# A fused transformer kernel on one core: where the first expert's weights are loaded

## The chip, the core and the metric

The kernel runs on one core of a Trainium2 chip. The metric is device time in microseconds (us). One execution was also recorded by the hardware profiler; every single event below comes from that execution. The engines are TensorE (PE: matmuls, PEld: its weight loads), VectorE (DVE), ScalarE (ACT), GpSimd (POOL) and SyncE (SP). SP here only issues weight loads; 16 DMA engines carry them out.

## What is computed

One hybrid layer on 256 tokens of width 1024, followed by a second block. In outline:

```python
proj = rmsnorm(x, g_mix) @ w_in
y_a = moba_attention(...)        # 8 heads
y_b = causal_attention(...)      # 8 heads, the "mla" branch
merged = sigmoid(gate_a) * (y_a @ w_branch_a) + sigmoid(gate_b) * (y_b @ w_branch_b)
x = x + merged @ w_out
x = x + routed_experts(rmsnorm(x, g_ffn), ...)   # 32 experts, top 4
x = x + sigmoid(rmsnorm(x, g_ple) @ w_ple_gate) * (p @ w_ple_proj)
# then a second block: swiglu, a mixer, memory attention, swiglu, rmsnorm
```

All weights are float32 in HBM. Each expert has 8 MB of gate-and-up weights and 4 MB of down weights, and all 32 experts are loaded, about 384 MB of the 544 MB that the kernel reads.

## The kernel before

The engines' programs are written out by hand, one function each (`tensor`, `scalar`, `vector`, `gpsimd`, `sync`), and run in the written order; semaphores tie them together. Weights are cut into **parts**: 1 MB each for the attention's matrices (`w_branch_a` and `w_branch_b` have two each, `w_out` four), 2 MB each for the experts (`gate_up` four parts, `down` two per expert).

`Plan.place` gives each part a place and makes the list of loads. There are five ring places of 2 MB, a place X behind them, a place Y in the work memory (both for experts only), and two odd ones: APART holds expert 0's fourth gate_up part in two pieces of 1 MB, ASIDE its first down part in pieces of 0.5 and 0.25 MB. A part goes to the place whose holder is the oldest. SP walks through the list in `load_before`: it waits until PE has used up the place's last holder (`pe["w", k]`), then issues the load. It is in order: a wait holds up every load behind it.

An attention part is not used as it lands. ACT first casts it to fp32r into the place's other half (`hi`, L1424), then DVE makes the rest (`lo`, L2012); PE needs both. ACT does this where its program says `hi_to(n)`, DVE at `lo_to(n)`. Parts 19, 20 and 21 are the second half of `w_branch_a` and the two of `w_branch_b`; parts 22 to 25 are `w_out`. Expert parts are used as they land.

The end of the attention goes, on PE: gate 3, branch_a 0, the transposes of the mla probabilities, branch_a 1 (L592 to L594), the mla values (L753, L754), branch_b 0, branch_b 1 with the transposes of the merged rows 0 and 1 (`merged_t`), out 0 (L611 to L613), out 1, the router. On ACT: `values` evacuates the mla values (L1466), `hi_to(24)` follows, then `merged_T(0)`, `merged_T(1)` (L1583). On DVE: `branch_b(0, h)`, `lo_to(22)`, `branch_b(1, 0)` (L2246, L2248), the rests of merged rows 0 and 1 (L2026). POOL waits for the mla values and then loads the experts' biases and the router (five transfers, 1 MB in all).

In the experts PE computes gate_up of expert n, then down of expert n-1. The load of an expert's part waits for a place that a part about 1.5 experts earlier gives up: the second gate_up part of expert 3 for the first of expert 2, for example.

Of the kernel before, what the change touches and what calls it, by code (L numbers as in the profile page):

```python
# [19 lines left out]
C_ID, C_CM, C_LT, C_NGE, C_ONE, C_IOTA, C_RC, C_RS, C_MC, C_MS, C_SEL, C_HM = (  # L20
    0, 128, 256, 384, 512, 640, 704, 768, 832, 864, 896, 928)
# [75 lines left out]
class Plan:  # L97
# [67 lines left out]
    def place(self):  # L165


        first, crowded, behind = (self.of[k][0] for k in (("gate_up", 0), ("gate_up", CHECK), ("ple_gate", 0)))
        self.apart, self.aside = self.of["gate_up", 0][3], self.of["down", 0][0]
        self.slot, self.at, self.loads = {}, {}, []  # L170
        count = dict.fromkeys(range(ASIDE + 1), 0)
        held = {s: s - NS for s in range(NS)}
        i = 0
        while i < len(self.parts):
            if i == first:
                held[X], held[Y] = self.of["out", 1][1] - 0.5, self.of["out", 1][1] + 0.5
            if i == crowded:
                del held[Y]
            if i == behind:
                del held[X]  # L180
            oldest = sorted(held, key=held.get)
            slots = oldest[:1]
            if i in (self.apart, self.aside):
                slots = [APART if i == self.apart else ASIDE]
            elif self.joined(i) and max(oldest[:2]) <= X and abs(oldest[0] - oldest[1]) == 1:
                slots = sorted(oldest[:2])
            after = [held[s] for s in slots if held.get(s, -1) >= 0]
            count[slots[0]] += {APART: 2, ASIDE: 5}.get(slots[0], 1) * 16
            for k, s in enumerate(slots):
                self.slot[i + k], self.at[i + k] = s, (slots[0], count[slots[0]])  # L190
                if s in held:
                    held[s] = i + k
            self.loads.append((i, len(slots), after))
            i += len(slots)
        early = next(n for n in self.loads if n[0] == self.apart)
        self.loads.remove(early)
        self.loads.insert(1 + [n[0] for n in self.loads].index(first), early)

    def on_vector(self, i):

# [47 lines left out]
def build(nc, d, out, known):  # L248
# [3 lines left out]
    with ExitStack() as ctx:  # L252
# [42 lines left out]
        def W(o, *shape):  # L295
            return view(Wt, o, shape)
# [47 lines left out]
        def raw_chunk(i, kk):  # L344

            if i == plan.apart:
                return (W(6144, 2048), W(10240, 2048))[kk]
            return chunks(raw(i), i)[:, kk, :]

        def down_half(i, kk, dh):  # L350
# [1063 lines left out]
        def scalar(e):  # L1414
            made = [0]

            def hi_to(i):

                while made[0] <= i:
                    j = made[0]  # L1420
                    made[0] += 1
                    if parts[j].split:
                        e.wait_ge(*in_memory(j))
                        e.copy(hi(j), raw(j)).then_inc(*act.now(("hi", j)))  # L1424
# [151 lines left out]
                probs_T("mla", g)  # L1576
            hi_to(21)
            values("mla", yT[1])
            hi_to(24)

            def merged_T(i):
                e.wait_ge(*pe["merged_t", i])
# [2 lines left out]

            for i in range(2):
                merged_T(i)
            hi_to(25)
            for i in (2, 3):
                merged_T(i)  # L1590
            e.wait_ge(bgu_in, 48)
            e.copy(bgub[0:96, :], bgu[0:96, :]).then_inc(*act.now("bias_hi"))
            e.activation(table_out, ident[:, 0:1], ACT.Sqrt).then_inc(*act.now("table0"))
            for q0 in (32, 64):
                e.wait_ge(*dve["bias_1", "rest"])
                e.copy(bgub[q0:q0 + 32, :], bgu[q0:q0 + 32, :]).then_inc(*act.now(("bias_1", q0)))
# [1265 lines left out]
        def sync(e):  # L2862
            e.dma_start(x[:, 0, :], d["x"][0:128, :]).then_inc(x_in0, 16)
            e.dma_start(x[:, 1, :], d["x"][128:256, :]).then_inc(x_in1, 16)
            made = [0]

            def load_before(i):

                while made[0] < len(plan.loads) and plan.loads[made[0]][0] < i:
                    j, n, after = plan.loads[made[0]]  # L2870
                    made[0] += 1
                    p, w = parts[j], d[parts[j].name]
                    for k in after:
                        e.wait_ge(*pe["w", k if k in plan.slot else of["out", 1][1]])
                    if p.name in PACKED:
                        src = w[p.c0 // p.n].rearrange("p (k n) -> p k n", k=p.k)
                    elif p.expert < 0:
                        src = rows(w, p.k0, p.k, p.c0, p.n)
                    elif p.name == "w_gate_up":
                        src = w[p.expert][p.k0 * 128:(p.k0 + p.k) * 128, :].rearrange("(p k) n -> p k n", p=128)  # L2880
                    else:
                        src = w[p.expert][p.k0 * 128:(p.k0 + p.k) * 128, :].rearrange("(p k) n -> p k n", p=128)
                    if j == 0:
                        e.dma_start(chunks(raw(0), 0)[:, 0:2, :], src[:, 0:2, :]).then_inc(first_in, 16)
                        e.dma_start(chunks(raw(0), 0)[:, 2:4, :], src[:, 2:4, :]).then_inc(loaded[0], 16)
                    elif j == plan.apart:
                        e.wait_ge(*pe["merged_t", 3])
                        for kk in range(2):
                            e.dma_start(raw_chunk(j, kk), src[:, kk, :]).then_inc(loaded[APART], 16)
                    elif j == plan.aside:  # L2890
                        e.wait_ge(*pe["logits"])
                        e.wait_ge(*act["bias_2", 64])
                        for k, v in enumerate((cst[:, C_HM:C_HM + 1024], W(12288, 1024), W(14336, 1024))):
                            e.dma_start(v, src[:, k, :]).then_inc(loaded[ASIDE], 16)
                        for c in range(2):
                            e.dma_start(aside[3][c], src[:, 3, c * 512:(c + 1) * 512]).then_inc(loaded[ASIDE], 16)
                    elif j == tail:
                        for k in range(3):
                            e.dma_start(chunks(raw(j), j)[:, k, :], src[:, k, :]).then_inc(tail_in[k], 16)
                        e.dma_start(chunks(raw(j), j)[:, 3, :], src[:, 3, :]).then_inc(in_memory(j)[0], 16)  # L2900
                    elif n == 2:
                        s = plan.slot[j]
                        e.dma_start(ring_t[:, s * SLOT:(s + 2) * SLOT].rearrange("p (k n) -> p k n", n=p.n),
                                    src).then_inc(in_memory(j)[0], 16)
                    else:
                        if plan.slot[j] == Y:
                            e.wait_ge(*pe["logits"])
                            e.wait_ge(*act["bias_2", 64])
                        e.dma_start(chunks(raw(j), j), src).then_inc(in_memory(j)[0], 16)
# [76 lines left out]
```

## Time and profile before

| | |
|---|---|
| median of 3 runs | 1754.18 us (1752.94 to 1755.97) |
| span of the profiled execution | 1754.0 us |
| PE busy | 1650.0 us (94%) |
| DMA moved | 546.39 MB, mean 312 GB/s |
| DMA rate in the 21 slices from 175 to 1096 us | 423 to 429 GB/s |
| chain that ended last | PE 48%, DMA 30% |

How to read the rows further down. A row of the stretches gives start:end and length, then busy us and instruction count of PE, PEld, DVE, ACT and POOL, the clock granted to PE (1.00 is 2.4 GHz, 0.50 is 1.2 GHz), the busy share of the DMA engines and their GB/s. A row of the timeline gives start, length, engine (SPq is SP's queue), line, operation, output<-input, shapes and count; idle time before it and what ended it stand in brackets. A row of the DMA issues gives output<-input, issuer, count, KB each and median us from issue to landing. A row of the waits gives who waited for whom, us in total, times, and the longest.

### The profile page before, as it was taken

To read this page: it belongs to the slowest core of one execution; us is meant where nothing else is said; L and a number is where in the kernel's file an instruction comes from. 1 tells how busy PE (TensorE), PEld (TensorE's weight loads), DVE (VectorE), ACT (ScalarE), POOL (GpSimd) and SP (SyncE) were. 2 spreads that over 40 slices of the span, in tenths; PEclk is the share of its full clock that TensorE was granted. 3 is DMA by queue.
4 is the path that set the end of the run, shared out by engine and by line. 5 is a ranking of instruction groups with operands and counts; after the bars stand their busy time and mean duration, and the time that the engine had idled before them with its cause. 6 is when DMAs were issued, how large, how long until landed. Compare 5 with 4: busy or idle time off the path is not lost.

```text
span 1754.0 us, 20351 instructions
## 1 busy us (share of the span) xinstructions
PE 1650.0 (94%) x8885; PEld 1037.7 (59%) x8886; DVE 705.4 (40%) x879; ACT 572.4 (33%) x790; POOL 24.5 (1%) x37
## 2 busy tenths in 40 slices
PE   9999999798889999988888888999999999999998
PEld 7788533342344544533232333388888998988886
DVE  5897411121212112111020111177664865567653
ACT  7576200111111111100000001175554765455552
POOL 1000000000000000000000000000000000000000
PEclk9999999999999999999999999999999999999999
DMA  7537999999999999999999999945555424445552
GB/s 250 171 120 294 424 423 429 426 427 428 428 426 427 428 426 427 426 427 428 429 427 427 429 424 428 400 159 192 192 192 172 164 97 135 164 136 179 191 192 96
DMA packets 119354, 546.39 MB, mean 312 GB/s; under 512 B 5776, under 2 KB 64272, under 8 KB 93696
## 3 DMA queue, kind: packets, MB, share of 16 engines
q1 hardware_dynamic: 117936, 540.96, 77.3%
q0 software_dynamic: 1040, 4.00, 0.7%
q8 instruction: 72, 1.18, 0.3%
q14 instruction: 18, 0.15, 0.0%
q10 hardware_dynamic: 288, 0.11, 0.0%
HBM read 544.00 MB, written 1.05 MB: 311 GB/s over the span
## 4 chain that ended last, share of the span: by engine, by line
PE 48%; DMA 30%; DVE 1%; ACT 1%; issue 1%; DVEq 0%; ACTq 0%
DMA ring<-in_w_down 30%; PE PS L1023 9%; PE PS L640 8%; PE PS L1182 6%; PE PS L647 4%; PE PS L982 2%; PE PS L625 1%; PE PS L626 1%; PE PS L627 1%; PE PS L1197 1%; PE PS L592 1%; PE PS L594 1%; PE PS L593 1%; PE PS L1225 1%; PE PS L664 1%; PE PS L666 1%
## 5 line engine op out<-in xcount | busy, mean ns | idle before, releaser
L982 PE MATMUL PS<-ring,work 128*64 128x512 f32 x1984 | 439.9, 595 | 29.8 <-DMA ring<-in_w_gate_up 29.7
L2012 DVE TENSOR_TENSOR ring<-ring,ring 128x2048 fp32r<-128x2048 f32 (+2 forms) x129 | 286.9, 2233 | 246.6 <-ACT ring L1424 246.5
L982 PEld LDWEIGHTS PS<-ring,work 128*64 128x64 f32 x1984 | 137.6, 137 | 311.9 <-issue 245.8
L1424 ACT CAST ring<-ring 128x2048 fp32r<-128x2048 f32 (+2 forms) x130 | 241.0, 1864 | 199.0 <-DMA ring<-in_mem_w_kv 85.5
L1023 PE MATMUL PS<-ring,work 128*64 128x512 f32 x992 | 235.7, 620 | 50.5 <-DMA ring<-in_w_down 35.8
L1023 PEld LDWEIGHTS PS<-ring,work 128*64 128x64 f32 x992 | 74.4, 141 | 197.0 <-issue 160.6
L2449 DVE TENSOR_SCALAR work<-PS 128x512 f32<-128x512 f32 x32 | 22.1, 690 | 321.0 <-PE PS L982 321.0
L1688 ACT ACTIVATE work<-work 128x512 f32<-128x512 f32 x32 | 20.2, 630 | 360.8 <-DVE work L2449 360.8
L2345 DVE TENSOR_TENSOR work<-PS,work 128x512 fp32r<-128x512 f32 x32 | 22.1, 692 | 253.7 <-ACT work L1631 253.7
L1182 PE MATMUL PS<-ring,work 128*128 128x512 f32 x432 | 98.2, 390 | 0.0
L1182 PEld LDWEIGHTS PS<-ring,work 128*128 128x128 f32 x432 | 81.2, 188 | 16.8
L640 PE MATMUL PS<-ring 128*128 128x512 f32 x320 | 75.2, 391 | 0.5 <-DVE ring L2503 0.5
L640 PE MATMUL PS<-work,ring 128*128 128x512 f32 x320 | 75.2, 391 | 0.5 <-DVE work L2503 0.5
L1631 ACT CAST work<-PS 128x512 fp32r<-128x512 f32 x32 | 18.8, 586 | 159.5 <-PE PS L1023 159.5
L640 PEld LDWEIGHTS PS<-work,ring 128*128 128x128 f32 x320 | 59.3, 188 | 13.0 <-DVE work L2503 1.4
L640 PEld LDWEIGHTS PS<-ring 128*128 128x128 f32 x320 | 59.3, 188 | 13.1 <-DVE ring L2503 1.4
L592 PE MATMUL PS<-ring 128*128 128x512 f32 (+1 forms) x160 | 62.9, 393 | 0.3
L593 PE MATMUL PS<-ring 128*128 128x512 f32 (+1 forms) x160 | 61.8, 386 | 0.0
L594 PE MATMUL PS<-ring 128*128 128x512 f32 (+1 forms) x160 | 61.8, 386 | 0.0
L924 PEld LDWEIGHTS PS<-work 128*128 128x128 f32 x256 | 34.0, 202 | 24.3 <-issue 23.5
L924 PE MATMUL PS<-work 128*128 128x256 f32 x256 | 40.3, 302 | 0.0
L647 PEld LDWEIGHTS PS<-ring 128*128 128x128 f32 x320 | 39.7, 192 | 0.8
(446 smaller groups left out, 2338.6 us busy)
## 6 DMA issues: line engine op xcount, KB each, us to landing
ring<-in_w_gate_up SPq DMA_DIRECT2D x124, 2048.0 KB, 21.6
ring<-in_w_down SPq DMA_DIRECT2D x61, 2048.0 KB, 21.4
ring<-in_ffn_w_gu SPq DMA_DIRECT2D x44, 1024.0 KB, 5.1
ring<-in_w_in SPq DMA_DIRECT2D x27, 1024.0 KB, 5.3
ring<-in_ffn_w_down SPq DMA_DIRECT2D x22, 1024.0 KB, 4.9
ring<-in_w_out SPq DMA_DIRECT2D x8, 1024.0 KB, 5.3
ring<-in_mem_w_kv SPq DMA_DIRECT2D x8, 1024.0 KB, 16.9
work<-in_w_gate_up SPq DMA_DIRECT2D x3, 2048.0 KB, 16.4
```

The costliest lines, as they stand in the source:

```text
L592: e.matmul(o, lT[0][:, k, hs], whi[:, kk, :], start=k == 0, stop=False, skip_group_check=True)
L593: e.matmul(o, lT[0][:, k, hs], wlo[:, kk, :], start=False, stop=False, skip_group_check=True)
L594: t = e.matmul(o, lT[1][:, k, hs], whi[:, kk, :], start=False, stop=k == nk - 1, skip_group_check=True)
L640: t = e.matmul(PS[:, bank + j, :], whi[:, k, j * 128:(j + 1) * 128], rT[2][:, :, k, :], start=first and k == 0, stop=not first and k == 7, ...
L647: t = e.matmul(PS[:, bank + j, 0:256], wlo[:, k, j * 128:(j + 1) * 128], rT[0][:, k, :], start=first and k == 0, stop=not first and k == 7 ...
L924: t = e.matmul(PS[:, bank, c * 256:(c + 1) * 256], half[:, h, 256 * i + c:256 * i + 256:2], PGr[:, h, :], start=h == 0 and z == 0, stop=h ...
L982: t = e.matmul(PS[hf * 64:hf * 64 + 64, bank, :], XG[g % 2][:, 2 * kp + kk, i * 64:(i + 1) * 64], raw_chunk(w, kk)[:, c0 + hf * 512:c0 + h ...
L1023: t = e.matmul(PS[dh * 64:dh * 64 + 64, BDN, :], HT[:, kk, kp * 64:kp * 64 + 64], down_half(w, kk, dh), start=kp == 0 and kk == 0, stop=kp ...
L1182: t = e.matmul(PS[:, 4 + 2 * h + nb, :], hT[z][:, c, hs], chunks(half, w)[:, kk, nb * 512:(nb + 1) * 512], start=c == 0 and q == 0, stop=F ...
L1424: e.copy(hi(j), raw(j)).then_inc(*act.now(("hi", j)))
L2012: e.tensor_tensor(lo(j), raw(j), hi(j).bitcast(F32), ALU.subtract).then_inc(*dve.now(("lo", j)))
L2345: e.tensor_tensor(YRl, PS[:, BDN, :], YRh.bitcast(F32), ALU.subtract).then_inc(*dve.now(("YR", n)))
```

## The change

Two of expert 0's gate_up parts, and pieces of two others, are loaded earlier, among the attention's last parts.

- `place` gives the two ring places that gate 2 leaves to expert 0's first two gate_up parts (4 MB). The attention's last seven parts (branch_a 1, branch_b 0 and 1, the four of w_out) turn over the three places that are left; each is loaded later than before.
- APART's two pieces are issued apart: piece 1 once the mla scores are done, ahead of branch_a 1's load; piece 0 after `merged_t` 3, ahead of the last w_out load. Piece 1 moves from W(10240) to W(10048).
- ASIDE's pieces: 0 and half of 3 without a wait ahead of expert 0's first load; 1 and 2 after the mla values and ahead of out 0's first load; the other half of 3 after the biases.
- ACT's `hi_to(24)` ahead of the merged rows becomes `hi_to(22)`; 23 and 24 come behind the two `merged_T` pairs, 25 behind the bias cast.

```diff
@@ place @@
+        begin, early = self.of["branch_a", 1][0], self.of["gate_up", 0][:2]
         while i < len(self.parts):
+            if i == begin:
+                for j in early:
+                    s = min(held, key=held.get)
+                    count[s] += 16
+                    self.slot[j], self.at[j] = s, (s, count[s])
+                    self.loads.append((j, 1, [held.pop(s)]))
             if i == first:
+                held.update((self.slot[j], j) for j in early)
+                i = early[-1] + 1
...
-        early = next(n for n in self.loads if n[0] == self.apart)
-        self.loads.remove(early)
-        self.loads.insert(1 + [n[0] for n in self.loads].index(first), early)
+        self.loads = [n for n in self.loads if n[0] not in (self.apart, self.aside)]
@@ scalar @@
             values("mla", yT[1])
-            hi_to(24)
+            hi_to(22)
...
             for i in range(2):
                 merged_T(i)
-            hi_to(25)
+            hi_to(23)
             for i in (2, 3):
                 merged_T(i)
+            hi_to(24)
             e.wait_ge(bgu_in, 48)
...
+            hi_to(25)
@@ sync @@
+            def beside_loads(j):
+
+                if j == of["gate_up", 0][0]:
+                    load_aside(0)
+                    load_aside(3, 0)
+                if j == of["branch_a", 1][0]:
+                    e.wait_ge(*pe["mla", "scores"])
+                    load_apart(1)
+                if j == of["out", 0][0]:
+                    e.wait_ge(*pe["mla", "values", 1])
+                    load_aside(1)
+                    load_aside(2)
+                if j == of["out", 1][1]:
+                    e.wait_ge(*pe["merged_t", 3])
+                    load_apart(0)
+                if j == of["down", 0][1]:
+                    e.wait_ge(*act["bias_2", 64])
+                    load_aside(3, 1)
```

SP's queue from the first load of branch_a to the last load of w_out. Before:

```order
L2909 DMA ring_49<-in_w_branch_a 128x4x512 [waits pe_attention_done] x2
L2909 DMA ring_49<-in_w_branch_b 128x4x512 [waits pe_attention_done] x2
L2909 DMA ring_49<-in_w_out 128x4x512 [waits pe_attention_done] x4
L2909 DMA ring_49<-in_w_gate_up 128x4096 [waits pe_attention_done]
L2889 DMA work_51<-in_w_gate_up 128x2048 [waits pe_attention_done]
L2889 DMA work_51<-in_w_gate_up 128x2048
L2909 DMA ring_49<-in_w_gate_up 128x4096 [waits pe_attention_done] x5
```

The same place in SP's queue after the change:

```order
L2942 DMA ring_49<-in_w_branch_a 128x4x512 [waits pe_attention_done]
L2887 DMA cst_55<-in_w_down 128x1024
L2889 DMA more_60<-in_w_down 128x512
L2942 DMA ring_49<-in_w_gate_up 128x4096 [waits pe_attention_done] x2
L2881 DMA work_51<-in_w_gate_up 128x2048 [waits pe_attention_done]
L2942 DMA ring_49<-in_w_branch_a 128x4x512 [waits pe_attention_done]
L2942 DMA ring_49<-in_w_branch_b 128x4x512 [waits pe_attention_done] x2
L2887 DMA work_51<-in_w_down 128x1024 [waits pe_attention_done]
L2887 DMA work_51<-in_w_down 128x1024
L2942 DMA ring_49<-in_w_out 128x4x512 [waits pe_attention_done] x3
L2881 DMA work_51<-in_w_gate_up 128x2048 [waits pe_attention_done]
L2942 DMA ring_49<-in_w_out 128x4x512 [waits pe_attention_done]
```

The expert loads have moved in among those of the attention, and the first three loads of w_out now stand behind a wait for the mla values and two pieces of w_down.

ACT from the evacuation of the mla values (L1466 before, L1473 after) to the bias cast; `ring0` read into `ring1` by a CAST is a `hi`, PS into `ring1` a merged row. Before:

```order
L1466 CAST work1_52<-PS 128x512 [waits pe_attention_done] x2
L1424 CAST ring1_50<-ring0_49 128x2048 [waits ring2_loaded]
L1424 CAST ring1_50<-ring0_49 128x2048 [waits ring3_loaded]
L1424 CAST ring1_50<-ring0_49 128x2048 [waits ring4_loaded]
L1583 CAST ring1_50<-PS 128x512 [waits pe_attention_done] x2
L1424 CAST ring1_50<-ring0_49 128x2048 [waits ring0_loaded]
L1583 CAST ring1_50<-PS 128x512 [waits pe_attention_done] x2
L1592 CAST work2_53<-work0_51 96x2048 [waits b_gu_loaded]
```

The same place on ACT after the change:

```order
L1473 CAST work1_52<-PS 128x512 [waits pe_attention_done] x2
L1431 CAST ring1_50<-ring0_49 128x2048 [waits ring1_loaded]
L1590 CAST ring1_50<-PS 128x512 [waits pe_attention_done] x2
L1431 CAST ring1_50<-ring0_49 128x2048 [waits ring2_loaded]
L1590 CAST ring1_50<-PS 128x512 [waits pe_attention_done] x2
L1431 CAST ring1_50<-ring0_49 128x2048 [waits ring3_loaded]
L1600 CAST work2_53<-work0_51 96x2048 [waits b_gu_loaded]
```

One cast of w_out is left ahead of the first two merged rows, in ring place 1; the others stand behind them. DVE's and PE's order is the same in both kernels.

## Rows read from the trace of the kernel before

**Rows 1.** The page's chain that ended last, share of the span by engine.

```profile
PE 48%; DMA 30%; DVE 1%; ACT 1%; issue 1%; DVEq 0%; ACTq 0%
```

**Rows 2.** The chain in order of time, start, length: one expert's wait.

```profile
392.07 26.92 DMA ring<-in_w_down
```

**Rows 3.** Stretches: PE, PEld, DVE, ACT, POOL busy; PE's clock; DMA share; GB/s.

```profile
120.00:145.00 25.00, 24.81 (x142) 20.72 (x141) 18.24 (x22) 19.73 (x44) 1.20 (x3) 1.00 0.47 166
145.00:150.00 5.00, 5.00 (x24) 4.12 (x23) 3.89 (x4) 4.55 (x3) 1.72 (x3) 1.00 0.90 222
...
160.00:180.00 20.00, 20.00 (x99) 16.70 (x97) 13.14 (x13) 11.78 (x15) 0.00 (x0) 1.00 1.01 429
200.00:240.00 40.00, 40.00 (x202) 15.63 (x200) 9.00 (x18) 4.04 (x8) 1.72 (x3) 1.00 1.01 429
...
241.00:246.00 5.00, 5.00 (x26) 1.64 (x24) 0.00 (x0) 0.00 (x0) 0.00 (x0) 1.00 0.99 374
...
400.00:500.00 100.00, 84.72 (x422) 31.30 (x420) 15.59 (x32) 12.62 (x25) 0.00 (x0) 1.00 1.01 427
```

**Rows 4.** PE's waits, total, times, longest: 100 to 186 us, then 186.7 to 336.

```profile
PE PS L910 <- DVE work L2318: 0.6, 1, 0.6
...
PE PS L1023 <- DMA ring<-in_w_down: 1.4, 2, 1.2
```

**Rows 5.** Timeline of SP's queue: start, length, what it issues.

```profile
127.20 0.37 SPq L2909 DMA_DIRECT2D ring<-in_w_branch_b  x1
...
155.78 0.34 SPq L2909 DMA_DIRECT2D ring<-in_w_gate_up  x1
...
162.15 11.21 SPq L2909 DMA_DIRECT2D ring<-in_w_gate_up  x3
...
241.39 0.33 SPq L2909 DMA_DIRECT2D ring<-in_w_gate_up  x1
```

**Rows 6.** DMA issues at 127.20, 143.80 to 144.80, 155.78 and 241.39: issue to landing.

```profile
ring<-in_w_branch_b SPq DMA_DIRECT2D x1, 1024.0 KB, 5.0
...
work<-in_b_gate_up POOLq DMA_DIRECT2D x3, 256.0 KB, 4.9
...
ring<-in_w_gate_up SPq DMA_DIRECT2D x1, 2048.0 KB, 7.6
...
ring<-in_w_gate_up SPq DMA_DIRECT2D x1, 2048.0 KB, 8.4
```

**Rows 7.** Timeline of ACT: the casts, the mla values, the merged rows.

```profile
128.53 1.98 ACT L1424 CAST ring<-ring 128x2048 fp32r<-128x2048 f32 x1
...
143.54 0.59 ACT L1466 CAST work<-PS 128x512 fp32r<-128x512 f32 x1 [0.72 <-PE PS L754]
144.02 5.53 ACT L1424 CAST ring<-ring 128x2048 fp32r<-128x2048 f32 x3
```

**Rows 8.** Timeline of DVE: rest of a part, branch_a 0, branch_b 1, merged rests.

```profile
130.55 2.29 DVE L2012 TENSOR_TENSOR ring<-ring,ring 128x2048 fp32r<-128x2048 f32 x1 [0.34 <-ACT ring L1424]
132.76 1.28 DVE L2229 TENSOR_TENSOR work<-PS,work 128x512 f32<-128x512 f32 x2
...
152.99 0.68 DVE L2246 TENSOR_TENSOR work<-PS,work 128x512 f32<-128x512 f32 x1
...
154.32 1.28 DVE L2026 TENSOR_TENSOR ring<-PS,ring 128x512 fp32r<-128x512 f32 x2
```

**Rows 9.** Timeline of PE: branch_a 1 begins; out 0 begins.

```profile
134.99 0.48 PE L592 MATMUL PS<-ring,work 128*128 128x512 f32 x1
...
155.59 0.39 PE L611 MATMUL PS<-ring 128*128 128x512 f32 x1
```

**Rows 10.** Timeline of PE, 16 matmuls each: after a short pause, after a long one.

```profile
498.12 3.65 PE L982 MATMUL PS<-ring,work 128*64 128x512 f32 x16 [1.24 <-DMA ring<-in_w_gate_up]
505.59 5.35 PE L1023 MATMUL PS<-ring,work 128*64 128x512 f32 x16 [3.81 <-DMA ring<-in_w_down]
```

**Rows 11.** Stretch right after that long pause, columns as in group 3.

```profile
507.00:510.20 3.20, 3.20 (x10) 1.20 (x8) 0.58 (x1) 0.00 (x0) 0.00 (x0) 0.50 1.02 435
```

More of the change, by code:

```diff
@@ L346, in raw_chunk @@
             if i == plan.apart:
-                return (W(6144, 2048), W(10240, 2048))[kk]
+                return (W(6144, 2048), W(10048, 2048))[kk]
             return chunks(raw(i), i)[:, kk, :]
@@ L2865, in sync, with rows_of, load_apart, load_aside @@
             made = [0]
+            def rows_of(j):
+                p = parts[j]
+                return d[p.name][p.expert][p.k0 * 128:(p.k0 + p.k) * 128, :].rearrange("(p k) n -> p k n", p=128)
+            def load_apart(kk):
+                e.dma_start(raw_chunk(plan.apart, kk), rows_of(plan.apart)[:, kk, :]).then_inc(loaded[APART], 16)
+            def load_aside(k, c=None):
+                src = rows_of(plan.aside)
+                if k < 3:
+                    v = (cst[:, C_HM:C_HM + 1024], W(12288, 1024), W(14336, 1024))[k]
+                    e.dma_start(v, src[:, k, :]).then_inc(loaded[ASIDE], 16)
+                else:
+                    e.dma_start(aside[3][c], src[:, 3, c * 512:(c + 1) * 512]).then_inc(loaded[ASIDE], 16)
+            def beside_loads(j):
[15 more added lines that the diff above has]
+                    load_aside(3, 1)
             def load_before(i):
@@ L2871, in load_before @@
                     made[0] += 1
+                    beside_loads(j)
                     p, w = parts[j], d[parts[j].name]
@@ L2885, in load_before @@
                         e.dma_start(chunks(raw(0), 0)[:, 2:4, :], src[:, 2:4, :]).then_inc(loaded[0], 16)
[L2886 to L2896, printed above, removed]
                     elif j == tail:
```

## The prediction

> **What bounds the kernel now.** I read the chain first, then the stretches, then the waits of PE and of SP's queue. The chain gives DMA 30% of the span [rows 1], in pieces like the 26.92 us of one expert at 392 us [rows 2]. The stretches say why: from 160 us on the 16 DMA engines are full and move 427 to 429 GB/s, while PE is idle for 15 of 100 us at 400 to 500 us [rows 3]. Before that, from 120 to 145 us, they move 166 GB/s [rows 3]. So a reader would start the expert stream earlier, in the attention's idle DMA time. At 427 GB/s 1 MB (1.049 million bytes) takes 2.46 us.
>
> But from when is the stream alone the bound? PE's waits answer: between 100 and 186 us it waits 0.6 us for one thing, and between 186.7 and 336 us only 1.4 us for a weight [rows 4]. Up to about 320 us PE is the one that runs without a pause, and loads go out when PE gives up places. I therefore look for the point where DMA has least queued work. A 2 MB load into a quiet queue takes 7.6 us (issued at 155.78), one that stands behind others takes more; the load issued at 241.39 took 8.4 us [rows 5, 6]. At 241.39 there was at most 0.8 us of queued work left (part of it a load of POOL's), although the stream had run for 85 us. The stretch from 241 to 246 us has 374 GB/s instead of 429 [rows 3]: a small hole is there already.
>
> **Part 1, the earlier stream.** The load at 241.39 goes out when PE has used up expert 2's first part, and this dependence isn't changed. If PE gets there at the same time, every byte that could be queued before is landed, and the stream restarts from that release whatever it had in hand. A lead of any size shrinks to the work that stood queued there: between nothing (the hole) and 0.8 us. I take a gain of 0.8 us. The 18 MB in nine places can be full sooner; nobody asks for them sooner. What the loads cost on SP is small: three more issues below 0.5 us each.
>
> It follows that PE's time of arrival in the experts counts in full. Any delay of PE in the attention moves the release at 241.39, and the DMA stream, then bound to the end of the experts, moves with it. So the rest is about PE in the attention, which had no slack there [rows 4].
>
> **Part 2, branch_a 1.** Its load was made long before; now it waits for gate 3's place, which comes free at 127.20 (where SP issued branch_b 1 before) [rows 5]. It lands 5.0 us later [rows 6], at 132.2. ACT stands at this cast at 128.53 already [rows 7] and holds its queue (the sigmoid of gate 3, the cast of branch_b 0, the probabilities). The cast takes 1.98 us, to 134.2; DVE's rest 2.29, to 136.5; then DVE has the first half of branch_a 0 to evacuate, 0.64 us [rows 8], and PE, which began at 134.99 [rows 9], begins at about 137.2. **+2.2 us.** The values, their evacuation (ACT at 143.54 [rows 7]) and branch_b move along: the values are done at 145.7.
>
> **Part 3, out 0.** SP now issues two 0.5 MB pieces after the mla values and only then out 0's first part; its own place is free earlier. Its landing is not shown by the trace. Lower bound: 2 MB from 145.8 in a quiet queue land in 7.6 us [rows 6], at 153.4. POOL issues its 1 MB at the same moment. In the trace these bytes had the engines to themselves and kept them 90% busy at 222 GB/s for most of 5 us [rows 3], the bias loads landing after 4.9 us [rows 6]. Shared at full rate they add 2.5 us, at their own rate 4.5 us: 155.9 or 157.9. I take 156.5, nearer the first, since mixed traffic at 241 us kept 374 GB/s.
>
> The rule that bears on this is in the Trainium skill, DMA: Bandwidth & Descriptors, Queues, rings and completion order: an engine takes turns between the queues that have work, packet by packet. By that rule POOL's megabyte delays out 0; by plain order of issue it would come behind and the landing would be 153.4.
>
> Now the queues behind it. ACT has this one cast ahead of the merged rows: 1.84 us (three took 5.53 [rows 7]). DVE has the rest of the part, 2.3 us, ahead of branch_b (1, 0), 1.33 us from its start to the merged rests, and the first merged rest is half of 1.28 us [rows 8]. With the hand-overs that is 6.3 us from landing to the start of out 0 on PE: 162.8 instead of 155.59 [rows 9]. **+7.2 us in all**, part 2's 2.2 included; with the bounds +4.1 and +8.6. Moving two casts behind the merged rows saves ACT 3.7 us, but only time that ACT had, since the rows waited for PE.
>
> **Part 4, the rest of out.** Out 0's second part can be loaded when branch_b 0 is done (about 151.7), out 1's first when branch_b 1 is (158): both are landed by 163, before PE wants them at 169 and 175. The last part waits for out 0's first (162.15 before [rows 5], now 170 to 171), so it is ready 5.1 + 1.9 + 2.3 = 9.3 us later, while PE has two parts ahead of it. Places came free every 5.4 us there (three issues from 162.15 within 11.21 us [rows 5]), so that is 10.9 us. It fits by 1.5 us; without this cover each further us of lateness would be one on PE. APART's second piece is issued 3 us ahead and is gone by then. I cost it at nothing. The router, the biases and place Y then come later along with PE.
>
> **Part 5, the clock.** PE stands still from the end of branch_b 1 at 157.7 to 162.8, about 5 us. After a pause of 3.81 us the trace shows the granted clock at 0.50 (1.2 GHz) for the next stretch [rows 10, 11], and 16 matmuls take 5.35 instead of 3.65 us: **+1.7 us**. Bounds: nothing, and 3.4 us if the 2.2 us pause of part 2 costs as much.
>
> **Sum.** 7.2 + 1.7 - 0.8 = +8.1 us on an execution of 1754.0 us, which lies 0.2 us under the median of 1754.18: **1762.3 us**. Since PE and the stream both move by this and nothing is changed after the first experts, it stays to the end.
>
> **Rivals.** (A) The stream is the bound from its start. Then 4 MB, APART's first piece and 0.75 MB of ASIDE leave it, and one w_out part (1 MB) comes in: 4.75 MB, 11.7 us, 1742.5 us. For it: 427 GB/s without a break from 160 us. Against: the latency of 8.4 us at 241.39, and PE without waits up to 320 us. A page backs it, the Trainium skill, Perfetto Trace Analysis, Optimization Strategy: a kernel with several regimes may gain when they are interleaved. By that rule the result is rival A; the trace agrees that there are two regimes, but also shows the places, not the engines, in charge between them. (B) The attention isn't delayed after all, because the late parts find PE still busy: then part 1 alone is left, 1753.4 us. For it speaks only that three places of 5.4 us work each are 16 us, more than the 9.3 us of load and casts; against, the wait for the values that stands ahead of out 0. (C) Out 0 lands at its lower bound and the clock stays up: +4.1 - 0.8, 1757.5 us. (D) POOL's bytes cost 4.5 us, both pauses cost clock and no backlog is won: +8.6 + 3.4 = +12, 1766.2 us. (E) The expected order doesn't bite, as the 4 MB themselves are issued late: they need gate 2's places, free at about 104 us, and land by 117, so this I exclude.
>
> **How the numbers follow.** Forecast 0.50, A 0.06, B 0.10, C 0.19, D 0.15. 0.2% is 3.5 us, about what a measurement of this kernel can tell from no change: within it fall B and about a third of C (its time lies just at the edge); faster is A. That gives faster 0.07, same 0.17, slower 0.76. The range takes in C and D, 1756.5 to 1767, and leaves out A, B and a little at each end, under 0.2.
>
> **What would show it.** (1) PE waits at branch_a 1 for DVE's rest, about 2 us, at 135. (2) PE waits at out 0 (about 5 us, on DVE's merged rest), and DVE and ACT wait there for the landing of w_out, 9 to 11 us after its issue near 146.8. (3) The clock is 0.50 for some us behind it. (4) DMA is idle for several us between 160 and 245, and the load of expert 3's second part goes out near 250 with a latency of about 7.6 us. (5) From there on everything stands 8 us later. I am wrong if out 0 starts before 160, or if a load goes out at 241 without a delay and the end still moves.

## The result, and the profile after

| | before | after |
|---|---|---|
| median, 4 runs each | 1753.76 us (1752.94 to 1755.97) | 1769.01 us (1768.42 to 1769.67) |
| span of the profiled execution | 1754.0 us | 1767.4 us |

The ratio is 1.0084, with a 95% interval of 1.0073 to 1.0096: the change costs 15.25 us, against 8.1 forecast. The direction was right and the size was not; 1769.0 lies above the range of 1756.5 to 1767.

The page's chain looks as it did [rows 1]:

```profile
PE 46%; DMA 31%; DVE 1%; ACT 1%; issue 0%; DVEq 0%; ACTq 0%
```

SP's queue through the attention's end, and the load that answers to the one at 241.39 [rows 5]. Columns as there:

```profile
127.21 0.38 SPq L2942 DMA_DIRECT2D ring<-in_w_branch_a  x1
...
147.33 0.83 SPq L2887 DMA_DIRECT2D work<-in_w_down  x2
148.20 0.43 SPq L2942 DMA_DIRECT2D ring<-in_w_out  x1
...
257.05 0.33 SPq L2942 DMA_DIRECT2D ring<-in_w_gate_up  x1
```

From issue to landing, for the loads at 127.21, 147.72, 148.20 and 257.05:

```profile
ring<-in_w_branch_a SPq DMA_DIRECT2D x1, 1024.0 KB, 5.0
...
work<-in_w_down SPq DMA_DIRECT2D x1, 512.0 KB, 11.0
...
ring<-in_w_out SPq DMA_DIRECT2D x1, 1024.0 KB, 13.9
...
ring<-in_w_gate_up SPq DMA_DIRECT2D x1, 2048.0 KB, 7.7
```

branch_a 1 behaves as a 1 MB load alone. Out 0's first part does not: 13.9 us for the same megabyte, landed at 162.1. The load at 257.05 goes out 15.66 us later than the one at 241.39 did and lands 14.9 us later; 7.7 us is the latency of a quiet queue [rows 6].

ACT stands in front of both late parts (timeline, as in group 7):

```profile
132.26 1.90 ACT L1431 CAST ring<-ring 128x2048 fp32r<-128x2048 f32 x1 [3.51 <-DMA ring<-in_w_branch_a]
...
147.34 0.59 ACT L1473 CAST work<-PS 128x512 fp32r<-128x512 f32 x1 [0.71 <-PE PS L761]
...
162.08 1.90 ACT L1431 CAST ring<-ring 128x2048 fp32r<-128x2048 f32 x1 [14.15 <-DMA ring<-in_w_out]
```

DVE's rest of that part, branch_b (1, 0) and the merged rests follow as in group 8:

```profile
164.01 2.29 DVE L2021 TENSOR_TENSOR ring<-ring,ring 128x2048 fp32r<-128x2048 f32 x1 [9.37 <-ACT ring L1431]
166.22 0.68 DVE L2255 TENSOR_TENSOR work<-PS,work 128x512 f32<-128x512 f32 x1
167.55 1.28 DVE L2035 TENSOR_TENSOR ring<-PS,ring 128x512 fp32r<-128x512 f32 x2
```

and PE starts branch_a 1 at 137.14 and out 0 at 168.38, where it had started at 134.99 and 155.59 [rows 9]:

```profile
137.14 0.50 PE L599 MATMUL PS<-ring,work 128*128 128x512 f32 x1 [1.90 <-DVE work L2238]
...
168.38 0.77 PE L618 MATMUL PS<-ring 128*128 128x512 f32 x1 [8.86 <-DVE ring L2035]
```

The first matmul takes 0.77 us instead of 0.39: the clock. The stretches of the kernel after, columns as in group 3:

```profile
138.00:141.30 3.30, 3.30 (x9) 2.59 (x8) 3.08 (x3) 3.30 (x6) 0.00 (x0) 0.50 0.00 0
...
150.00:158.00 8.00, 8.00 (x42) 6.69 (x40) 3.53 (x5) 0.00 (x0) 0.52 (x1) 1.00 1.01 249
...
168.40:172.00 3.60, 3.60 (x9) 2.83 (x10) 3.56 (x4) 0.00 (x0) 0.00 (x0) 0.50 0.00 0
...
199.40:206.20 6.80, 6.25 (x28) 4.34 (x29) 5.59 (x16) 2.60 (x4) 1.55 (x2) 0.50 1.00 425
...
400.00:500.00 100.00, 86.10 (x438) 33.43 (x436) 21.42 (x45) 15.58 (x32) 1.71 (x3) 1.00 1.01 427
```

Three stretches at half clock (1.2 GHz), one behind each pause and one in the router. Between 120 and 250 us the kernel before had only the last, and half as long:

```profile
186.00:189.30 3.30, 3.30 (x14) 2.57 (x13) 2.52 (x6) 1.39 (x2) 1.54 (x2) 0.50 0.99 420
```

From 150 to 158 us the engines are full (share 1.01) at 249 GB/s; in the same kernel they are as full at 427 GB/s from 400 on. And that last row is the row of before [rows 3]: in the steady part nothing has changed. So the whole loss is made before 206 us. In steps, each the difference of the two traces: branch_a 1 +2.15, the mla values +3.8 (ACT's evacuation at 147.34 instead of 143.54), out 0 +12.8, the release of expert 3's second gate_up part +15.7, its landing +14.9. The spans differ by 13.4, the medians by 15.25. A span is about 1.8 us shorter than the time of its execution (1767.4 for 1769.17 after), so the profiled execution of the kernel before took some 1755.8 us, 2 us above its median. It has a half-clock stretch at the end of the experts (16 matmuls in 5.35 us at 1119.82) where the same 16 took 3.65 us after, which is 1.7 us of this.

### The profile page after: what moved, and what is told of

Same layout as the page of the kernel before. It is cut to its first block, busy times and chain, and to the rows that moved or that the text cites. A ratio compares the mean times of both kernels' runs of the same rounds, so it can differ in the third digit from the quotient of the medians.

```text
span 1767.4 us, 20350 instructions
## 1 busy us (share of the span) xinstructions
PE 1647.5 (93%) x8885; PEld 1037.5 (59%) x8886; DVE 705.7 (40%) x879; ACT 572.7 (32%) x790; POOL 24.6 (1%) x37
## 3 DMA queue, kind: packets, MB, share of 16 engines
HBM read 544.00 MB, written 1.05 MB: 308 GB/s over the span
## 4 chain that ended last, share of the span: by engine, by line
PE 46%; DMA 31%; DVE 1%; ACT 1%; issue 0%; DVEq 0%; ACTq 0%
DMA ring<-in_w_down 31%; PE PS L1030 9%; PE PS L647 8%; PE PS L1189 6%; PE PS L654 4%; PE PS L989 2%; PE PS L632 1%; PE PS L633 1%; PE PS L634 1%; PE PS L1204 1%; PE PS L599 1%; PE PS L601 1%; PE PS L600 1%; PE PS L1232 1%; PE PS L671 1%; PE PS L673 1%
## 5 line engine op out<-in xcount | busy, mean ns | idle before, releaser
L989 PE MATMUL PS<-ring,work 128*64 128x512 f32 x1984 | 441.6, 597 | 34.8 <-DMA ring<-in_w_gate_up 34.8
L2021 DVE TENSOR_TENSOR ring<-ring,ring 128x2048 fp32r<-128x2048 f32 (+2 forms) x129 | 287.0, 2234 | 271.5 <-ACT ring L1431 271.3
L1030 PE MATMUL PS<-ring,work 128*64 128x512 f32 x992 | 226.9, 600 | 51.2 <-DMA ring<-in_w_down 37.8
L647 PE MATMUL PS<-ring 128*128 128x512 f32 x320 | 75.2, 391 | 0.5 <-DVE ring L2512 0.5
L647 PEld LDWEIGHTS PS<-ring 128*128 128x128 f32 x320 | 59.2, 188 | 13.1 <-DVE ring L2512 1.4
L618 PE MATMUL PS<-ring 128*128 128x512 f32 x80 | 32.4, 405 | 10.4 <-DVE ring L2035 8.9
```

The lines of the kernel that those rows point to most:

```text
L618: e.matmul(o, lT[0][:, k, hs], whi[:, kk, :], start=k == 0, stop=False, skip_group_check=True)
L647: t = e.matmul(PS[:, bank + j, :], whi[:, k, j * 128:(j + 1) * 128], rT[2][:, :, k, :], start=first and k == 0, stop=not first and k == 7, ...
L989: t = e.matmul(PS[hf * 64:hf * 64 + 64, bank, :], XG[g % 2][:, 2 * kp + kk, i * 64:(i + 1) * 64], raw_chunk(w, kk)[:, c0 + hf * 512:c0 + h ...
L1030: t = e.matmul(PS[dh * 64:dh * 64 + 64, BDN, :], HT[:, kk, kp * 64:kp * 64 + 64], down_half(w, kk, dh), start=kp == 0 and kk == 0, stop=kp ...
L2021: e.tensor_tensor(lo(j), raw(j), hi(j).bitcast(F32), ALU.subtract).then_inc(*dve.now(("lo", j)))
```

## The experiments

The theory: the loss is PE's delay in the attention, carried over by the release at 241.39, and the lead of the early bytes is worth nothing there. The rivals: the stream itself bounds (a lead counts, a delay of PE is absorbed); or the turning over of three places costs the time, not the wait and the pieces ahead of out 0. Every run is compared with the kernel before on the same chip. "Release" is the issue of expert 3's second gate_up part, 241.39 before and 257.05 after.

**1. Only a delay of PE.** The kernel before, with products of zeros for some 10 us ahead of the experts.

```diff
             tok_part(xT, of["out", 1], 1, 1, PS[:, 3, :], ("out", 1, 1))
+            idle_products(7, 44)
             pe.stage("experts")
```

> The kernel before, with 44 products of zeros (about 0.23 us each, 10.0 us together, bank 7, results unused) on PE between the last w_out matmul and the router. No load, place or order is changed. Theory T (from PE's arrival in the experts on, loads go out as PE gives up places, and the stream has under 1 us of queued work at 241 us): the whole kernel is later by 10.0 less 0 to 0.8 us, +9.2 to +10.0 us; the load of 241.39 goes out near 251 with a latency near 7.6 us. Rival (the stream of weights is the bound from 160 us on): PE's 10 us are hidden, within +-1 us of the kernel before.

1764.0 us, ratio 1.0055 (1.0038 to 1.0071), +9.9 us. SP's queue and the landing of the released load:

```profile
251.97 0.33 SPq L2910 DMA_DIRECT2D ring<-in_w_gate_up  x1
...
ring<-in_w_gate_up SPq DMA_DIRECT2D x1, 2048.0 KB, 8.0
```

The release moved by 10.6 us, the end by 9.9. The full queue of loads absorbed nothing. This is the step that the forecast rested on, and it stands.

**2. The wait and the two pieces away from out 0.** After, with both moved behind `merged_t` 3.

```diff
-                if j == of["out", 0][0]:
-                    e.wait_ge(*pe["mla", "values", 1])
-                    load_aside(1)
-                    load_aside(2)
                 if j == of["out", 1][1]:
                     e.wait_ge(*pe["merged_t", 3])
+                    load_aside(1)
+                    load_aside(2)
                     load_apart(0)
```

> The changed kernel, but the wait for the mla values and the two 0.5 MB pieces of w_down stand behind merged_t 3 (with APART's piece) instead of ahead of out 0's first load. Theory T: out 0's first part goes out at about 145 and lands at 150 to 152, PE doesn't wait at out 0; what is left is the pause at branch_a 1 and its clock loss, 3.6 us, less up to 0.8: +2.8 to +3.6 us against the kernel before. Rival (three places are too few, whatever stands ahead of out 0): still +8 us or more.

1761.2 us, ratio 1.0040 (1.0026 to 1.0054), +7.1 us. Half of the loss is gone, but not as much as expected, a miss. Out 0's first part landed after 5.0 us. PE's waits from 100 to 200 us show why: DVE's rest at L2021 is that of w_out's last part, which was now queued behind 2 MB of pieces. My edit had made a wait of its own.

```profile
PE PS L618 <- DVE ring L2021: 2.6, 1, 2.6
PE PS L599 <- DVE work L2238: 2.3, 1, 2.3
```

**3. The same, with the pieces behind all of w_out.**

```diff
-                if j == of["out", 0][0]:
-                    e.wait_ge(*pe["mla", "values", 1])
+                if j == of["gate_up", 0][2]:
+                    e.wait_ge(*pe["merged_t", 3])
                     load_aside(1)
                     load_aside(2)
-                if j == of["out", 1][1]:
-                    e.wait_ge(*pe["merged_t", 3])
                     load_apart(0)
```

> As out_unblocked (+7.1 us), but the two pieces of w_down and APART's piece 0 stand behind w_out's last load, which had PE waiting 2.97 us there. Theory T (only PE's pauses and the clock after them count): the pause at branch_a 1 is left, 2.2 + 1.4 us, less up to 0.8: +2.8 to +3.6 us. Rival (three places cost more than their pauses): still +7 us.

1757.9 us, ratio 1.0020 (1.0011 to 1.0030), +3.6 us. Only the pause at branch_a 1 is left:

```profile
PE PS L599 <- DVE work L2238: 1.8, 1, 1.8
```

So the part of the loss at out 0 is 15.3 - 3.6 = 11.7 us. What half clock adds is in this difference: the trace of this run has none behind the pause at branch_a 1, after has. The release is at 243.89, 2.5 us late.

**4. Without the early 4 MB.** After, with `early` empty: the seven parts have all five places.

```diff
-        begin, early = self.of["branch_a", 1][0], self.of["gate_up", 0][:2]
+        begin, early = self.of["branch_a", 1][0], []
...
-                i = early[-1] + 1
```

> The changed kernel without its early 4 MB: expert 0's first two parts stand at their old place in the list and attention has five places again; the pieces, SP's waits and ACT's order stay as in the change. Theory T (the wait for the mla values and the 1 MB ahead of out 0 make the delay): out 0's first part is issued at about 144.5 and lands near 158; PE begins out 0 near 164.5, 9 us late, plus 1.9 us of clock, less 0.8: +10 us. Rival (the turning over of three places makes it): PE isn't late, within 1 us of the kernel before.

1765.9 us, ratio 1.0072 (1.0055 to 1.0089), +11.8 us. The pause at branch_a 1 is gone, out 0's first part still took 14.2 us, and PE waited for it:

```profile
PE PS L617 <- DVE ring L2034: 9.2, 1, 9.2
```

The three places don't make the delay of out 0; the wait for the values and the pieces do. 11.8 here and 3.6 in experiment 3 add up to the whole, 15.3.

**5. Each of the two suspects at out 0 apart.** First POOL's megabyte moved out of the way, behind the first merged rows:

```diff
             e.wait_ge(*pe["mla", "values", 1])
+            e.wait_ge(*pe["merged_t", 1])
             for i in range(3):
```

> The changed kernel with POOL's five loads (1 MB) behind merged_t 1 instead of at the mla values. Their sharing of the engines is out of the way of out 0. Theory T: the three loads issued from 147.3 on land as 2 MB in a quiet queue do, after 7.6 to 8.1 us (162.06 in the changed kernel), PE begins out 0 near 162 instead of 168.4: +9 us against the kernel before. Rival (the two pieces of w_down and the w_out part are slow by themselves): still about +15 us.

1762.5 us, ratio 1.0054 (1.0039 to 1.0070), +8.0 us. Out 0's load, issued at 146.83, and PE's wait for it:

```profile
ring<-in_w_out SPq DMA_DIRECT2D x1, 1024.0 KB, 8.2
...
PE PS L618 <- DVE ring L2035: 3.2, 1, 3.2
```

It lands at 155.0 instead of 162.1. From the first of the three issues that is 9.1 us instead of 14.7: POOL's 1 MB alone had cost out 0 5.6 us. The kernel ends 7.3 us earlier. Some 1.4 us of that isn't POOL's: in this execution the stretch behind the pause at branch_a 1 is at full clock, and the mla values are done earlier by as much (first issue at 145.96 instead of 147.33).

Then the wait kept where it is, and only the two pieces moved behind `merged_t` 3:

```diff
                     e.wait_ge(*pe["mla", "values", 1])
-                    load_aside(1)
-                    load_aside(2)
                 if j == of["out", 1][1]:
                     e.wait_ge(*pe["merged_t", 3])
+                    load_aside(1)
+                    load_aside(2)
                     load_apart(0)
```

> The changed kernel with SP's wait for the mla values kept ahead of out 0, but the two 0.5 MB pieces behind merged_t 3. Theory T: out 0's part is issued at 147.3, with POOL's 1 MB beside it; at the 0.25 MB/us seen when both ran together it lands near 158, 4 us sooner than in the changed kernel: +11 us. Rival (the wait alone is the cost, the 1 MB ahead costs nothing): +15 us.

1769.5 us, ratio 1.0085 (1.0070 to 1.0101), +15.0 us, a miss. Out 0's part landed 9.6 us after its issue, and the pause ahead of it did shrink: PE began out 0 at 162.2, 6 us earlier than after. But the pieces stood ahead of w_out's last part again, as in experiment 2, and PE paused there:

```profile
PE PS L618 <- DVE ring L2035: 3.7, 1, 3.7
PE PS L618 <- DVE ring L2021: 2.6, 1, 2.6
```

The trace has three half-clock stretches, beginning at 160.7, 184.6 and 198.2 us. Together with the second pause they go with most of the 6 us; the release is only 1.1 us earlier than after. By its total alone the run would speak for "the pieces cost nothing"; the waits say otherwise. It also shows the traffic. The stretch from 151 to 155 us, and the queues in it (q0 is POOL's, q1 is SP's; packets, MB, share of the engines' busy time):

```profile
151.00:155.00 4.00, 4.00 (x21) 3.29 (x20) 1.56 (x3) 0.00 (x0) 0.00 (x0) 1.00 1.00 195
```

```profile
q0 software_dynamic: 164, 0.75, 95.1%
q1 hardware_dynamic: 15, 0.02, 4.7%
```

These 195 GB/s are POOL's transfers almost alone, and they keep the engines full. Of SP's part, issued at 146.3, 1.02 of 1.05 million bytes had moved by 151, at 408 GB/s between 149 and 150, when it had the engines to itself. Its last packets took the next 4 us (15 packets, 0.02 MB), and it counts as landed only with them. The same stretch of pool_late, with POOL's loads out of it:

```profile
151.00:155.00 4.00, 4.00 (x22) 3.36 (x21) 1.38 (x2) 0.00 (x0) 0.00 (x0) 1.00 0.96 354
```

So each of the two suspects makes out 0's part late. From the first issue to its landing it took 5.0 us with neither (experiment 2), 9.1 with the pieces ahead of it, 9.6 with POOL's megabyte beside it, and 14.7 with both.

**6. The clock's share.** After, with products of zeros in place of the pause ahead of out 0.

```diff
+            idle_products(7, 36)
             tok_part(xT, of["out", 0], 0, 0, PS[:, 0, :], ("out", 0, 0), [dve["mergedT", i] for i in range(2)])
```

> The changed kernel with 36 products of zeros (8.3 us, results unused) on PE ahead of out 0, in the pause that it has there anyway. Nothing else is changed. Theory T (part of the +15 us is half clock after the pause, not the wait itself): out 0's first 12 matmuls take 2.7 instead of 4.6 us and the half clock at the router gets shorter: 1.9 to 3.5 us less than the changed kernel, +11.7 to +13.4 us. Rival (the clock costs nothing, DVE's rests come late anyway): +15 us.

1765.0 us, ratio 1.0070 (1.0055 to 1.0086), +10.5 us. The clock stays up where it had been 0.50:

```profile
158.00:172.00 14.00, 12.95 (x63) 7.71 (x63) 9.21 (x10) 6.23 (x7) 0.00 (x0) 1.00 0.52 187
```

PE still waits 1.0 us for the rest, and the weights land no sooner (13.8 us after their issue). The kernel ends 4.8 us earlier than after, more than forecast, and its release is 4.1 us earlier. But 1.4 of these 4.1 us stand already at the mla values (145.96 against 147.33), ahead of the added products, which can't have made them: in this execution the stretch at 138 us is at full clock too, although its pause was the same 1.9 us. The 12 matmuls of out 0 took 2.7 instead of 4.6 us, and the router's half clock lasted 3.4 instead of 6.8 us. So the run shows some 2.8 us for the clock behind the pause at out 0 and in the router. Six of the kernels here have the pause of about 2 us at branch_a 1; two of their traces, after and out_unblocked, have half clock behind it and four have none. I can't say from these runs when it comes.

**7. Is the lead worth anything when PE isn't delayed?** The kernel before, with its own places for the attention, but with 2.75 MB of the pieces issued early, ahead of the last w_out load, and `hi_to(25)` behind the bias cast.

```diff
+                if j == of["out", 1][1]:
+                    load_aside(0)
+                    load_aside(3, 0)
+                    e.wait_ge(*pe["mla", "scores"])
+                    load_apart(1)
+                    e.wait_ge(*pe["mla", "values", 1])
+                    load_aside(1)
+                    load_aside(2)
+                if j == of["gate_up", 0][1]:
+                    e.wait_ge(*pe["merged_t", 3])
+                    load_apart(0)
...
```

> The kernel before, with 2.75 MB loaded early and nothing of the attention's loads held up by more than that: no early 4 MB; ASIDE's two free pieces, APART's piece 1 and ASIDE's pieces 1 and 2 go out behind out 1's first load (140.7 us) and ahead of its second; APART's piece 0 and ASIDE's last stay late. ACT casts w_out's last part behind the bias cast. Theory T (what the stream has in hand at 241 us is lost, PE isn't delayed): 0 to -0.8 us against the kernel before. Rival A (every MB moved out of the stream is 2.46 us): -6.7 us.

1754.3 against 1754.5 us, ratio 1.0001 (0.9992 to 1.0010). 2.75 MB are 6.8 us of streaming, and nothing of it arrives:

```profile
241.34 0.33 SPq L2937 DMA_DIRECT2D ring<-in_w_gate_up  x1
...
ring<-in_w_gate_up SPq DMA_DIRECT2D x1, 2048.0 KB, 8.1
```

The release is where it was, and the load lands after 8.1 us as before. Where the lead goes can be seen in the stretch at the release [rows 3]:

```profile
241.00:246.00 5.00, 5.00 (x26) 1.68 (x24) 0.00 (x0) 0.00 (x0) 0.00 (x0) 1.00 0.75 261
```

The engines are 75% busy there at 261 GB/s, where they were 99% busy at 374 before: less work stands queued, SP's and POOL's, since some of it had been moved before. These 2.75 MB are the part of the change that costs nothing.

Then the counter-test: if the release is what swallows the lead, the lead must show once places come free earlier. Both kernels, with half of expert 0's gate_up products left out (7.3 us of PE):

```diff
-                    for kk in range(2):
+                    for kk in ((1,) if n == 0 else range(2)):
```

The kernel before, cut in this way:

> The kernel before; half of the gate_up products of expert 0 are left out (32 matmuls, 7.3 us of PE), all loads stay. PE gives up the places of experts 1 and 2 about 7.3 us earlier. Theory T: the stream is full from 156 us on in this kernel, so it gains only what it idled and lacked at 241 us, 0.3 to 1.5 us: -0.3 to -1.5 us. Rival (PE's pace alone decides): -7.3 us.

1753.7 us, ratio 0.9997 (0.9988 to 1.0006). The kernel with the early pieces, cut in the same way:

> pieces_only (2.75 MB early at no cost to PE, +0.0 us) with the same 32 matmuls of expert 0 left out. Theory T: now the places come free in time for the lead to be kept: up to 2.75 MB, 6.7 us, at most 7.3 us: -5.5 to -7.3 us against the kernel before, 5 to 6 us under before_short. Rival (early bytes are worth nothing here for another reason): the same time as before_short.

1750.9 us, ratio 0.9982 (0.9972 to 0.9991), 2.8 us faster than the other, half of the 5 to 6 forecast. The release is at 234.26 without the lead and at 235.05 with it; from issue to landing, a line of each kernel:

```profile
ring<-in_w_gate_up SPq DMA_DIRECT2D x1, 2048.0 KB, 15.8
```

```profile
ring<-in_w_gate_up SPq DMA_DIRECT2D x1, 2048.0 KB, 10.5
```

Now 15.8 and 10.5 us mean that work stands queued. Without the lead, 7.3 us less of PE bring only 0.6 us: the stream is the bound. With the lead the load lands at 245.6 instead of 250.1. That is 4.5 us and not 6.8, and most of what is missing was missing by 160 us already: from 120 to 160 us the kernel with the pieces moved 8.87 million bytes against 7.15, 1.7 more and not 2.9, and 1.7 are 4.0 us at 427 GB/s. Both kernels then ran the engines full. The early pieces had shared the time from 150 to 155 us with POOL's loads, at 250 GB/s. Of the 4.5 us the median shows 2.8; where the rest goes is not shown.

**8. Three attempts at the 4 MB without delay of PE.** The 4 MB take places from branch_b 0 on instead of from branch_a 1 on; the pieces as in experiment 2 (first attempt), or behind w_out with the 4 MB issued behind branch_b 1 (second), and POOL's loads behind `merged_t` 1 as well (third).

```diff
-        begin, early = self.of["branch_a", 1][0], self.of["gate_up", 0][:2]
+        begin, early = self.of["branch_b", 0][0], self.of["gate_up", 0][:2]
```

> The changed kernel with the pieces of w_down moved as in out_unblocked, and expert 0's first two parts put in behind branch_a 1 instead of ahead of it, so that branch_a 1 keeps its early load. The early 4 MB stay early. Theory T: PE arrives as in the kernel before, the stream restarts from the same release: 0 to -0.8 us. Rival A (a stream that starts with 4.75 MB in hand ends 11.7 us earlier): -11.7 us.

1764.5 us, ratio 1.0061 (1.0044 to 1.0078): the 4 MB now stood ahead of branch_b's two parts, and PE paused 4.0 us at the mla values and 2.5 us at out 1. Second:

```diff
+        moved = [n for n in self.loads if n[0] in early]
+        self.loads = [n for n in self.loads if n[0] not in early]
+        at = 1 + [n[0] for n in self.loads].index(self.of["branch_b", 1][0])
+        self.loads[at:at] = moved
```

> The changed kernel rearranged so that the 4 MB are early and PE isn't held up: the two early parts take the places that gate 2 and gate 3 leave, but SP issues them (and APART's piece 1) behind branch_b 1's load; branch_a 1 keeps its early load; out 0 has no wait for the mla values; all other pieces stand behind w_out's last load. Theory T (a lead is lost at the release of 241 us): if PE begins out 0 within 1 us of 155.6, 0 to -0.8 us against the kernel before, plus whatever PE is late. Rival A (4 MB and APART's piece in hand, 5 MB): -12 us.

1766.5 us, ratio 1.0071 (1.0057 to 1.0085): the 4 MB, and APART's piece 1 behind them, now stood ahead of out 0's part, which took 18.7 us:

```profile
ring<-in_w_out SPq DMA_DIRECT2D x1, 1024.0 KB, 18.7
...
PE PS L622 <- DVE ring L2039: 10.0, 1, 10.0
```

Third:

> early_4mb_clean (+12.2 us) with POOL's five loads behind merged_t 1. w_out's first part is issued at 141 behind 5 MB, lands near 151 instead of 159.6, and PE begins out 0 within 1 us of 155.6. Theory T (a lead is lost at the release of 241 us): 0 to -0.8 us against the kernel before. Rival A (5 MB in hand): -12 us.

1762.4 us, ratio 1.0042 (1.0028 to 1.0056): 13.6 us for that part, and a pause of 4.9 us. None of the three is the kernel I wanted. But each gives another pair of numbers, and the last has 4 MB in place early and still ends 8.0 us late with its release 7.0 us late.

All runs with their whole work. The delay of the release is read from the trace, that of the end from the medians:

| kernel | release later by | end later by |
|---|---|---|
| pieces_only | 0.0 | -0.2 |
| out_unblocked_2 | 2.5 | 3.6 |
| pool_late | 6.6 | 8.0 |
| clean_pool_late | 7.0 | 8.0 |
| out_unblocked | 7.9 | 7.1 |
| early_4mb_no_stall | 8.2 | 10.4 |
| pe_late_10 | 10.6 | 9.9 |
| clock_kept | 11.5 | 10.5 |
| no_early_4mb | 12.1 | 11.8 |
| early_4mb_clean | 12.8 | 12.2 |
| wait_only | 14.5 | 15.0 |
| after | 15.7 | 15.3 |

The two columns go together within about 2 us, with 4 MB loaded early or without, with 2.75 MB or without. The delay at the release is the result.

## Why the prediction was half right

**The bound and the lead (part 1): right.** The stream restarts from the release at 241.39, and what it had in hand is gone. Experiment 1 shows the delay going through, experiment 7 the lead vanishing, and its second half the lead coming back when the places come free earlier. The 0.8 us that I credited for the backlog are inside the noise of all this. (I also set the span of the profiled execution beside the median of the times, 0.2 us under it; a span is 1.8 us shorter than its time. Nothing rests on it.) Rivals A (a lead of 4.75 MB) and B (no delay) fall with it.

**branch_a 1 (part 2): right.** 2.15 us late against 2.2 forecast.

**From landing to PE (part 3, second half): right.** Landed at 162.1, out 0 on PE at 168.38: 6.3 us, as worked out from the casts and rests.

**The landing of out 0 (part 3, first half): the step that failed.** I had it at 156.5, 10.7 us after the first of the three issues; it was 14.7 us, and it started from values that were themselves 1.6 us later than I had them, because the 2.15 us pause had 3.4 us at half clock behind it. Both terms of the sum that gave the landing were too small. I took the two pieces and the part as 2 MB in a quiet queue, 7.6 us; without POOL they took 9.1 (experiment 5). They also began slowly: from 147 to 149 us in that run SP's queue, alone, moved 215 GB/s. And I took POOL's megabyte as 3.1 us, between 2.5 and 4.5; it was 5.6 us (14.7 - 9.1). My bounds added its bytes to SP's, as if SP's own kept their full rate beside them. They don't: from 154 to 158 us after, both queues together move 231 GB/s on full engines, where SP's alone moves 406 GB/s in pool_late (151 to 153 us). "Nearer the first, since mixed traffic at 241 us kept 374 GB/s" leaned on another load: POOL's traffic from 241 to 246 us is 0.52 MB of `mem`, moved in 26% of the engines' busy time, thus at near full rate, and not the biases and the router.

The rule that I quoted from the Trainium skill (DMA: Bandwidth & Descriptors, Queues, rings and completion order), that an engine takes turns between its queues, held in its direction: out 0 was delayed by POOL's loads. From 148 to 160 us SP's queue had 61% of the engines' busy time and POOL's 35%, so neither waited for the other to end. How even the turns are, no run here shows.

**The rest of out (part 4): right for this kernel.** No wait at w_out's last part after the change. Experiments 2 and 5 show how thin the cover was: 1 MB more ahead of it, and PE paused 2.6 us, against 1.5 us of cover in the forecast.

**The clock (part 5): right in kind, mis-sized.** 1.7 us forecast. In the trace of after it is 1.6 us behind the first pause, which I had only as a bound, 1.85 behind the second, and up to 1.7 in the router, where 3.4 us at 0.50 became 6.8. The last I hadn't looked for. Experiment 6 confirms the second and the third together (2.8 us); the first came and went between runs with the same pause. The router's stretch isn't tied to the change alone either: it lasted 6.8 us in pe_late_10 too, where PE has no pause in the attention.

Summed by the trace of after, up to the release: 2.15 for branch_a 1, 1.6 for the clock behind it, 9.05 for the landing of out 0 (12.8 - 2.15 - 1.6, against 5.0 forecast), 1.85 for the clock behind that, and 1.0 that is left, for the router: 15.7. So the landing carries 4 of the missing 7 us and the clock most of the rest. Rival D had the right places and sizes that were still too small (+12).

**What stays open.** Why POOL's biases and router weights move at about half rate even when they have the engines to themselves (236 GB/s from 147 to 149 us before), why SP's are slowed beside them, and why a pause of 2 us costs clock in some executions and not in others. Whether the 4 MB could be early at no cost to PE: not shown, since each attempt delayed something else. Experiment 7 suggests that it wouldn't pay if they were, but it had 2.75 MB early and not 4.

No kernel with all its work was faster than the kernel before; the nearest, pieces_only, can't be told from it.

## What to carry to other kernels

Before you load something earlier, find the next point at which the stream waits for a place to come free, and read the time from issue to landing there: if it is that of a quiet queue, a lead is lost at that point and only a delay gets through. Count every transfer that runs beside a load which an engine waits for, from all queues, and not just the added ones; take for all of them together the slowest rate that the trace shows while they run. Here 1 MB ahead of the load and 1 MB beside it cost 4 to 6 us each, where 2.46 is what a megabyte takes at full rate. And when an experiment moves a load out of the way, look first at what now stands behind it; five of these kernels had a wait that I had put there.

## What the runs showed of the chip that I had not expected

- POOL's 1 MB of biases and router weights kept the engines full at 195 to 236 GB/s almost alone; SP's w_out loads alone moved 406 GB/s in the same place. Side by side the two made 231 to 249 GB/s.
- A load lands with its last packet: beside POOL's traffic SP's part had moved 1.02 of 1.05 million bytes in 4.7 us and landed 9.6 us after its issue.
- The same 1 MB load took 5.0 us alone, 8.2 behind 1 MB of its own queue, 9.6 with POOL's 1 MB beside it, 13.9 with both, 13.6 behind 5 MB and 18.7 behind 5 MB and beside POOL.
- Pauses of PE of about 2 us were followed by a stretch at the granted clock of 0.50 in two of six kernels, and the one of 8.9 us ahead of out 0 by 3.6 us at 0.50 once PE ran again. Filling the longer pause with products of zeros took 4.8 us off the end; 2.8 of the 4.1 us at the release can be laid to it.
- A half-clock stretch in the router was 3.4 us long before and 6.8 us after, with no change in the work there; in before_short the router had none.
